# Hymba decoder block on one core: fewer places for TensorE's small products, states accumulated in PSUM, the diagonal blocks moved by nine transfers

## What is computed

```python
sa = -einsum('bhvk,bhk->bhv', S, kk_t)
S = S * w_t + sa[..., None] * b_t + v_t[..., None] * k_t
y = einsum('bhvk,bhk->bhv', S, r_t)
```

## Time and profile before

| | |
|---|---|
| median of three runs | 2065.28 us (2063.19 to 2066.71) |
| the profiled execution | 2057.9 us, its span 2056.1 us |
| TensorE | 1959.0 us busy, 15982 products |
| VectorE | 1251.0 us (61%) |
| ScalarE | 767.4 us (37%) |
| GpSimd | 369.9 us (18%) |
| DMA, hardware queue | 165456 packets, 32.5% of 16 engines |
| granted TensorE clock | 0.988 of full speed |

### The profile page before, as it was taken

How to read it: one execution, slowest core, us unless ns; L and a number is a source line. 1 busy time by engine, 2 the same in 40 slices (tenths; PEclk the granted TensorE clock), 3 DMA queues, 4 the chain that set the end, 5 groups by cost and what they waited for, 6 DMA issues and landing times.

```text
span 2056.1 us, 40076 instructions
## 1 busy us (share of the span) xinstructions
PE 1959.0 (95%) x15982; PEld 1549.3 (75%) x15982; DVE 1251.0 (61%) x2416; ACT 767.4 (37%) x1438; POOL 369.9 (18%) x672
## 2 busy tenths in 40 slices
PE   8999999999999998999999999999999899999995
PEld 5777777777777876777777777777777677887883
DVE  5657576675756676665757666675767655336434
ACT  6443334342424243434333424242424342334321
POOL 0001303021212121022131303121212122110112
PEclk9999999999999999999999999999999999999997
DMA  5532222222232224322222222222232433446443
GB/s 166 179 87 79 71 84 74 76 70 85 61 94 72 72 77 130 105 77 67 83 71 82 67 78 75 80 65 84 67 86 75 131 94 104 128 146 209 158 122 108
DMA packets 165643, 197.36 MB, mean 96 GB/s; under 512 B 70096, under 2 KB 73168, under 8 KB 165456
## 3 DMA queue, kind: packets, MB, share of 16 engines
q1 hardware_dynamic: 165456, 194.79, 32.5%
HBM read 174.79 MB, written 19.92 MB: 95 GB/s over the span
## 4 chain that ended last, share of the span: by engine, by line
PE 54%; DVE 11%; SPq 11%; POOL 10%; DMA 8%; issue 4%; ACT 2%; DVEq 0%; ACTq 0%; POOLq 0%
PE psum L1113 43%; SPq L358 6%; POOL xt L457 4%; POOL x L455 4%; SPq L353 3%; DMA x<-scratch_L 2%; SPq L337 2%; PE psum L1266 2%; DVE w_lo L695 2%; DMA w_raw<-in_w_in 2%; DMA scratch_X<-xt 2%; DMA scratch_L<-late 1%; ACT w_hi L513 1%; PE psum L1373 1%; DVE late L857 1%
## 5 line engine op out<-in xcount | busy, mean ns | idle before, releaser
L1113 PE MATMUL psum<-x_hi,w_hi 128*128 128x512 f32 x2144 | 895.1, 418 | 10.2 <-DVE x_lo L704 7.6
L1113 PE MATMUL psum<-x_hi,w_lo 128*128 128x512 f32 x2144 | 843.0, 393 | 0.0
L1113 PE MATMUL psum<-x_lo,w_hi 128*128 128x512 f32 x2144 | 840.3, 392 | 0.0
L513 ACT ACTIVATE w_hi<-w_raw 128x512 fp32r<-128x512 f32 x536 | 335.9, 630 | 1079.8 <-PE psum L1113 1003.9
L695 DVE TENSOR_TENSOR w_lo<-w_raw,w_hi 128x512 fp32r<-128x512 f32 x456 | 318.7, 700 | 504.1 <-ACT w_hi L513 488.6
L1113 PEld LDWEIGHTS psum<-x_hi,w_hi 128*128 128x128 f32 x2144 | 405.8, 189 | 129.2 <-issue 31.6
L1113 PEld LDWEIGHTS psum<-x_hi,w_lo 128*128 128x128 f32 x2144 | 404.9, 189 | 89.9
L1113 PEld LDWEIGHTS psum<-x_lo,w_hi 128*128 128x128 f32 x2144 | 406.3, 190 | 78.8 <-issue 7.7
L493 POOL TENSOR_TENSOR w_lo<-w_raw,w_hi 128x512 fp32r<-128x512 f32 x80 | 102.8, 1286 | 510.3 <-ACT w_hi L513 510.3
L953 DVE SCALAR_TENSOR_TENSOR states<-psum,pc,pt 128x64 f32<-128x64 f32 x112 | 31.7, 283 | 117.4 <-PE psum L1373 116.9
L449 POOL COPY xt<-sub_ident 64x256 f32<-64x256 f32 x16 | 6.3, 392 | 506.4 <-DMA x<-scratch_L 506.4
(11 more groups left out here) (240 smaller groups left out, 2035.7 us busy)
## 6 DMA issues: line engine op xcount, KB each, us to landing
w_raw<-in_w_in SPq DMA_DIRECT2D x408, 256.0 KB, 2.7
w_raw<-in_w_out SPq DMA_DIRECT2D x128, 256.0 KB, 2.6
stage<-in_x_t SPq DMA_DIRECT2D x20, 256.0 KB, 3.5
stage<-scratch_MIX SPq DMA_DIRECT2D x19, 256.0 KB, 4.0
x_t<-scratch_X SPq DMA_DIRECT2D x256, 4.0 KB, 1.6
scratch_MIX<-sa SPq DMA_DIRECT2D x16, 256.0 KB, 3.1
scratch_MIX<-ym SPq DMA_DIRECT2D x16, 256.0 KB, 3.4
lora<-in_x_t SPq DMA_DIRECT2D x16, 256.0 KB, 3.0
```

The lines of the kernel that those rows point to most:

```text
L513: return nc.scalar.activation(dst, src, ACT.Copy, scale=scale)
L1113: mm = nc.tensor.matmul(psum[:, s % 2], wt[gq % SPLIT][:, cols], xx[:, c], start=(c == 0 and wt is w_hi and xx is x_hi), stop=(c == KC - 1 ...
```

## The change

- `products` 0 moves from the middle of step 0 to step 1, in front of `products` 1, and the LoRA products of `channels` from step 2 to 1. `z` moves from step 6 to 5 behind the scores, level 0 from 12 to 11 behind the first values, `values` 1 from 15 to 14 in front of level 1, and level 2 from 15 to 14 behind it, into banks 2 and 3 (it waits for `kk_read`, their last reader, and no longer for level 1).
- VectorE masks both halves in step 1, ahead of the recurrence; its `level` 2 moves to step 14; the centring of y (`centre`) to the end of step 24.
- The fresh part stays in bank 6 unscaled. Each `chain` product adds to its columns there, and ScalarE (`chain`, an ACTIVATE with the scale `pc`) makes the next state: odd m ahead of `high`, even m behind it. `fresh`, `n_full`, `fresh_ready` and L939 go.
- Scratch `L`, `X` and a new `XT` hold whole 64x64 blocks with a gap of one row, so that `diagonal` addresses the 16x16 blocks as 64 rows of one stride. Transfers: 2 out, 1 in, 2 out, 4 back. Ahead of the loop four transfers write zeros to `X` and `XT`.
- All low parts are VectorE's.

```diff
@@ -265,13 +268,14 @@
-def pool_low(gq):
-    return any(j >= 1 and 19 <= at < 24 for j, at in current(gq - 4))
-def lows(gq, by_pool):
-    return sum(pool_low(x) == by_pool for x in range(gq + 1))
+def whole(name):
+    return scr[name].rearrange("(m r) -> m r", r=BLOCK_STEP)[:, 0:C * C].rearrange("m (s t) -> m s t", t=C)
+def diagonal(name):
+    places = scr[name].rearrange("(p r) -> p r", r=BLOCK_STEP * SUB // C)[:, 0:SUB * C]
+    return places.rearrange("p (s t) -> p s t", t=C)[:, :, 0:SUB]
@@ -290,8 +294,7 @@
             if gq >= RAW:
-                done = gq - RAW
-                sp.wait_ge(w_ready_pool if pool_low(done) else w_ready, lows(done, pool_low(done)))
+                sp.wait_ge(w_ready, gq - RAW + 1)
@@ -330,33 +333,28 @@
                 sp.wait_ge(a_read, 2 * i + 2)
-                for f in range(P // SUB):
-                    c = 1 if f < 4 else 0
-                    rows = slice(f * SUB, (f + 1) * SUB)
-                    cols = slice((f % 4) * SUB, (f % 4 + 1) * SUB)
-                    sp.dma_start(scr["L"][f].rearrange("m s t -> s m t"),
-                                 am[rows, :, :, c, 1 - c, cols].rearrange("s b h t -> s (b h) t")
+                for c in range(2):
+                    sp.dma_start(whole("L")[BH * c:BH * (c + 1)].rearrange("m s t -> s m t"),
+                                 am[us_rows(c), :, :, c, 1 - c].rearrange("s b h t -> s (b h) t")
...
-                sp.wait_ge(l_out, 8 * 16 * (i + 1))
+                sp.wait_ge(l_out, 2 * 16 * (i + 1))
...
-                sp.dma_start(sub_l, scr["L"].rearrange("f m s t -> (f m) s t")).then_inc(l_in, 16)
+                sp.dma_start(sub_l, diagonal("L")).then_inc(l_in, 16)
...
-                sp.dma_start(scr["X"].rearrange("f m x s t -> (f m) x s t"), sub_x).then_inc(x_out, 16)
+                if i == 0:
+                    sp.wait_ge(x_zero, 4 * 16)
+                sp.dma_start(diagonal("X"), sub_x[:, 0]).then_inc(x_out, 16)
+                sp.dma_start(diagonal("XT"), sub_x[:, 1]).then_inc(x_out, 16)
...
-                sp.wait_ge(x_out, 16 * (i + 1))
-                sp.wait_ge(pool_inited, 1)
-                for f in range(P // SUB):
-                    rows = slice(f * SUB, (f + 1) * SUB)
-                    cols = slice((f % 4) * SUB, (f % 4 + 1) * SUB)
-                    sp.dma_start(x16[rows, :, cols], scr["X"][f, :, 0].rearrange("m s t -> s m t")
+                sp.wait_ge(x_out, 2 * 16 * (i + 1))
+                for c in range(2):
+                    sp.dma_start(x16[us_rows(c)], whole("X")[BH * c:BH * (c + 1)].rearrange("m s t -> s m t")
...
-                    c = 1 if f < 4 else 0
-                    for hh in range(2):
-                        rows = slice(hh * HD + (f % 4) * SUB, hh * HD + (f % 4 + 1) * SUB)
-                        sp.dma_start(x16_t[rows, NB * c:NB * (c + 1), cols],
-                                     scr["X"][f, hh::2, 1].rearrange("b s t -> s b t")).then_inc(x_back, 16)
+                for hh in range(2):
+                    sp.dma_start(x16_t[head_rows(hh)], whole("XT")[hh::2].rearrange("m s t -> s m t")
+                                 ).then_inc(x_back, 16)
@@ -407,6 +405,11 @@
         load_up(1)
+        sp.wait_ge(pool_inited, 1)
+        for c in range(2):
+            for name in ("X", "XT"):
+                sp.dma_start(whole(name)[BH * c:BH * (c + 1)].rearrange("m s t -> s m t"), x16[us_rows(c)]
+                             ).then_inc(x_zero, 16)
@@ -640,6 +637,12 @@
+        def chain(i, m):
+            act.wait_ge(state_full, NCH * i + m + 1)
+            dst = states[:, m + 1] if m < NCH - 1 else state[:, i % PAIRS]
+            copy(dst, psum[:, 6, m * HD:(m + 1) * HD], pc[:, i % 2, m:m + 1]).then_inc(state_new, 1)
@@ -662,8 +665,14 @@
         for gq in range(QUARTERS):
+            for j, at in current(gq):
+                if j >= 1 and 21 <= at < 25:
+                    chain(j - 1, 2 * (at - 21) + 1)
...
+            for j, at in current(gq):
+                if j >= 1 and 20 <= at < 24:
+                    chain(j - 1, 2 * (at - 20))
@@ -907,7 +916,7 @@
             for x in range(2):
-                part_ = psum[:, (6, 6, 6, 4, 6)[lev] + x, 0:NB * C].rearrange("p (b t) -> p b t", b=NB)
+                part_ = psum[:, (6, 6, 2, 4, 6)[lev] + x, 0:NB * C].rearrange("p (b t) -> p b t", b=NB)
@@ -935,10 +943,6 @@
             dve.sem_inc(mt_ready, 1)
-            dve.wait_ge(n_full, i + 1)
-            then(nc.vector.tensor_tensor(fresh, psum[:, 6].rearrange("p (m d) -> p m d", d=HD),
-                                         pc[:, j].unsqueeze(2).broadcast_to([P, NCH, HD]), ALU.mult))
-            dve.sem_inc(fresh_ready, 1)
@@ -946,19 +950,15 @@
-        def chain(i, m):
-            n = i % PAIRS
-            dve.wait_ge(state_full, NCH * i + m + 1)
-            dst = states[:, m + 1] if m < NCH - 1 else state[:, n]
-            then(nc.vector.scalar_tensor_tensor(dst, psum[:, 7, 0:HD], pc[:, i % 2, m:m + 1], fresh[:, m],
-                                                ALU.mult, ALU.add))
-            dve.sem_inc(state_new, 1)
+        def centre(i):
+            spread = [P, BH, HD]
+            then(nc.vector.tensor_reduce(stat[:, 0], ym[:], AX, ALU.add))
+            then(nc.vector.tensor_scalar(stat[:, 0], stat[:, 0], -1.0 / HD, None, ALU.mult))
+            then(nc.vector.tensor_tensor(ym[:], ym[:], stat[:, 0].unsqueeze(2).broadcast_to(spread),
+                                         ALU.add))
+            dve.sem_inc(y_centred, 1)
...
-            if at == 0:
-                masked(i, 0)
-            if at == 1:
-                masked(i, 1)
@@ -976,8 +976,8 @@
                 level(i, 1)
+                level(i, 2)
...
-                level(i, 2)
@@ -993,10 +993,6 @@
                 transition(i)
-            if 21 <= at < 25:
-                chain(i, 2 * (at - 21) + 1)
-            if 20 <= at < 24:
-                chain(i, 2 * (at - 20))
@@ -1066,16 +1055,23 @@
         for gq in range(QUARTERS):
-            if gq + 4 < QUARTERS and not pool_low(gq + 4):
+            if gq + 4 < QUARTERS:
...
+                if j >= 1 and at == 1:
+                    masked(j - 1, 0)
+                    masked(j - 1, 1)
+            for j, at in current(gq):
...
+            for j, at in current(gq):
+                if j >= 1 and at == 24:
+                    centre(j - 1)
@@ -1101,7 +1097,7 @@
                 pe.wait_ge(tile_read, s - 1)
-            pe.wait_ge(w_ready_pool if pool_low(gq) else w_ready, lows(gq, pool_low(gq)))
+            pe.wait_ge(w_ready, gq + 1)
@@ -1123,7 +1119,7 @@
         def channels(j, at):
-            if at == 2:
+            if at == 1:
@@ -1272,12 +1268,12 @@
         def recurrence(i, at):
             if at == 1:
+                products(i, 0)
                 products(i, 1)
             if at == 3:
                 turns(i)
             if at == 5:
                 scores(i, 0)
-            if at == 6:
                 pe.wait_ge(t_read, 4 * i + 4)
                 mm = from_chunks(4, lambda b, c, hh: am[vs_rows(c), b, hh, c, 1 - c],
                                  lambda b, c, hh: uv[vs_rows(c), c, b, hh])
@@ -1287,19 +1283,18 @@
                 scores(i, 1)
             if at == 11:
                 values(i, 0)
-            if at == 12:
                 pe.wait_ge(s_read, 2 * i + 2)
-                pe.wait_ge(x_back, 24 * 16 * (i + 1))
+                pe.wait_ge(x_back, 4 * 16 * (i + 1))
                 from_chunks(6, masked_l, lambda b, c, hh: x16[us_rows(c), 2 * b + hh]).then_inc(lev_full, 1)
             if at == 13:
                 turn_p(i, 1)
             if at == 14:
+                values(i, 1)
                 pe.wait_ge(lev_read, 5 * i + 1)
                 from_heads(6, ym, x16_t).then_inc(lev_full, 1)
-            if at == 15:
-                values(i, 1)
-                pe.wait_ge(lev_read, 5 * i + 2)
-                from_heads(6, x16_t, ym).then_inc(lev_full, 1)
+                if i < INTERVALS - 1:
+                    pe.wait_ge(kk_read, i + 2)
+                from_heads(2, x16_t, ym).then_inc(lev_full, 1)
             if at == 16:
                 pe.wait_ge(lev_read, 5 * i + 3)
                 pe.wait_ge(mixa_ready, 2 * i + 2)
@@ -1332,8 +1327,8 @@
                                                   kbt[:, b, c, rows], uv[:, c, b, hh],
-                                                  start=True, stop=True, skip_group_check=True)
-                mm.then_inc(n_full, 1)
+                                                  start=(b == 0 and c == 0), stop=False,
+                                                  skip_group_check=True)
@@ -1366,12 +1361,10 @@
                 pe.wait_ge(mt_ready, i + 1)
-                pe.wait_ge(h_read, i + 1)
-                pe.wait_ge(fresh_ready, i + 1)
...
-            nc.tensor.matmul(psum[:, 7, 0:HD], mt[:, m], states[:, m], start=True, stop=True
-                             ).then_inc(state_full, 1)
```

(6 more changed lines are left out.)

24 lines of the change are left out of this document (5 added, 19 removed).

## The result

The median after is **1980.4 us** (1978.17 to 1982.50, 4 runs) against 2065.1 (2063.19 to 2066.71, 4 runs) before: ratio 0.959, 95% interval 0.9573 to 0.9607, so 84.7 us gained. Forecast were 2004.3 and the range 1990 to 2029; the kernel is faster, and faster than the range allowed. The profiled execution took 1980.56 us (span 1978.8, granted clock 0.991), 77.3 us less than that of before.

The account below looks back on a forecast made before the run. TensorE, busy 95% of the span, was taken as the bound. In us, joins 24.5, waits 22.9 + 3.6 + 2.4 and borders 8, less 0.4 at the start, made 61 off 2065.3: 2004.3, range 1990 to 2029.

Parts of the forecast that it names:

- joins: TensorE's small groups moved beside neighbours: 0.37 us saved in one tile shape, 0.21 across shapes, 24.5 us in all.
- borders: At the two changes to a new half of x, fewer TensorE waits for VectorE's states: 8 us, bounds 0 and 18.
- rival 1: Waits come back elsewhere, VectorE nearly full in steps 12 to 14, inverse norm tight before step 12's transposes: 2026, chance 0.12.
- 22.9 + 3.6 + 2.4: TensorE's waits that go, in us: level 0 for its transfer, turn of step 13, level 2 for level 1's reader.
- taking off the same 61 from 2065.3: Last step: the gain worked out on the profiled run (2057.9 us) applied to the median, giving 2004.3.
- 11 x 0.33 = 3.6: Turn of step 13: eleven waits for `softmax_norm` go, as the weight load no longer stands behind 24 issues: 3.6 us.
- Step 9, put at nothing: The other 16 `softmax_norm` waits, at step 9, hang on ScalarE's exponentials and stay.
- Level 2: At step 14, no longer waits for level 1's reader but for `kk_read`: 2.4 us gained, 5 us cost at worst.
- The landing: Returned blocks: 11.5 us earlier by fewer issues, less 3 for larger transfers; 3 us of cover before level 0.
- it fits: ScalarE's queue takes the chain's states, perhaps 0.3 us each, around the high part: nothing on TensorE.
- The low parts: nothing: Steps 19 to 23: VectorE takes over 80 low parts, 0.70 us each, without its state steps: no effect.
- The interval: Each of the 16 intervals expected 3 to 4 us shorter.

Follow-up runs that it names:

- experiment 1: The kernel before with only the nine new transfers (scratch layout, issues and waits of the change): 2015.8 us, ratio 0.9759.
- 2: The changed kernel with all joins undone, the six groups at their old steps, transfers and states as changed: 2000.9 us, ratio 0.9691.
- the first lot: The timing lot in which runs of the kernel before stood beside four of the follow-up kernels; before's median there was 2065.4 us.
- experiment 8: The changed kernel with step 9 reordered, scores of the second half ahead of the turned probabilities of the first: 1972.2 us, ratio 0.9568.
- experiment 5: The changed kernel with the chain's states back on VectorE, the low parts staying there too: 2010.4 us, ratio 0.9745.
- experiment 4: The changed kernel with the old 34 transfers instead of the nine: 2059.3 us, ratio 0.9962.
- 6: The changed kernel with the five low parts of steps 19 to 23 back on GpSimd: 1980.9 us, ratio 0.9608.
- experiment 7: The changed kernel with the states back on VectorE and the five low parts back on GpSimd: 1989.0 us, ratio 0.9654.

## Why the prediction missed

| term | forecast | distances | medians |
|---|---|---|---|
| transfers: level 0, turn 13, level 2 | 28.9 | 38.1 (before, 1) | 49.6 |
| joins | 24.5 | 22.3 (2, after) | 20.5 |
| borders, start, all else | 7.6 | 11.6 (1, 2) | 14.9 |
| outside the groups: the clock | 0 | 5.3 | |
| before's median above its profiled run | 0 | 7.4 | |
| sum | 61 | 84.7 | 85.0 |

(In brackets the two kernels compared. The medians' column goes from 2065.4, before in the first lot, over 2015.8 and 2000.9 to 1980.4.)

Nearly every mechanism of the forecast was there, and no rival came (the tight fit that rival 1 named shows only in the kernel of experiment 8). The time missed the forecast by 23.9 us, and 20.7 of them are in one row, the transfers.

- **The step that failed is the price of the waits for the transfers, "22.9 + 3.6 + 2.4".** It takes a us of waiting in the table for a us of time. Experiment 1 took these waits away alone: 38.1 us by the distances and 49.6 by the medians, for 28.9. Of the 38.1, level 0 is 24.7 for 22.9, turn 13 is 6.8 for 3.6, level 2 is 3.0 for 2.4, and step 9, which was said to stay, is 2.8. A wait costs more than its length even at the full clock: 0.2 us more at step 13 (experiment 1), less than 0.1 at level 2 (0.30 us for 0.23 to 0.24), 0.26 in the chain of experiment 5 (0.48 us for 0.22). And behind some of the long ones TensorE runs at the lower clock.
- **The clock.** Before, some of TensorE's waits for level 0 were followed by stretches at 1.2 GHz; its timeline:

```profile
664.01 0.69 PE L1257 MATMUL psum<-x,late 64*64 64x64 f32 x32 [2.03 <-DMA x_t<-scratch_X]
...
666.12 0.63 PE L1113 MATMUL psum<-x_hi,w_hi 128*128 128x512 f32 x1
666.55 0.63 PE L1113 MATMUL psum<-x_lo,w_hi 128*128 128x512 f32 x1
```

  The large products are 0.43 us apart instead of 0.23, after four of the sixteen waits (2.0 to 2.4 us long), and after none of the twelve others (0.35 to 1.76). That waits bring such stretches is shown by experiments 1 and 4: outside the groups there are 39 spacings at half the clock before, 15 with the waits gone (experiment 1, none of them at a level 0) and 84 with longer waits (experiment 4, clock 0.979). How often it happens differs from run to run: the 13 runs of before in the first lot spread from 2059.3 us (granted clock 0.990) to 2073.3 (0.984), and the slower ones have the lower clock. With the wait gone the four runs lie within 4.3 us at 0.990 to 0.991, and the profiled one is at the median. The prediction's last step, "taking off the same 61 from 2065.3", took the 7.4 us between the profiled run (2057.9, 0.988) and the median for something that both kernels have. They are gone after the change. About 4 us of them are the clock by an estimate (the median clock of the 13 runs is 0.986: 0.002 x 2057); the rest is open, and medians of the same kernel differed by up to 5 us between the lots. So 5 us are the clock in the profiles, and perhaps 4 more in the medians.
- **"11 x 0.33 = 3.6".** The eleven waits make 4.1 us, so the reading was near. What it left out is the 0.2 us on top of each; the groups of step 13 fell by 6.8.
- **Step 9, put at nothing.** The prediction said that its sixteen waits hang on ScalarE's exponentials and stay. They made 12.0 us before (one of them below), 9.1 with the nine transfers, 7.8 after the whole change and 9.4 when the old transfers came back (experiment 4), so they hung on the transfers in part. By what way is open.

```profile
987.39 1.09 PE L1098 MATMUL psum<-cst,score 128*128 128x128 f32 x8 [0.82 <-DVEq L897]
```

- **Level 2, the right size for the wrong reason.** Its wait of 2.4 us went with the transfers alone (experiment 1), with the old banks and the old reader. That it waits for `kk_read` now gained nothing that a run shows, and cost nothing: at most 0.3 us an interval was feared, and its group costs 2.32 to 2.34 us in nearly every interval.
- **The joins**: 0.37 for one shape against 0.40 (12.7 / 32) and 0.33 (5.2 / 16); 0.21 across shapes against 0.20 for `z`. Level 0 behind the values gave 0.12: it had stood beside the transposes of step 12, and the four interruptions fewer were counted, the old neighbour was not. The extrapolation from 64x64 to 64x128 tiles, which no row showed, held.
- **The landing**: 11.5 us saved less 3 for the larger transfers, and 3 us of cover, were forecast. The cover was 3.6 us, but two misses cancel in it. In the interval of the rows, the time from the first issue of the blocks to the last landing fell from 1001.75 - 963.09 = 38.7 us to 953.9 - 922.45 = 31.5, so 7.2 earlier: the larger transfers took 4.3 of the 11.5, not 3. In return the blocks leave 1.1 us earlier before level 0 is asked for (957.51 - 922.45 = 35.1 us, against 997.1 - 963.09 = 34.0), for which the sum had nothing.
- **The states**: "it fits", at 0.3 us each. 313 ns, no wait of a chain product, spacing 1.60. "The low parts: nothing" is right as well (6), and for the reason given, that VectorE has no state steps there any more: with them it costs 15 to 21 us (experiment 5 against 7).
- **The borders**: 8 forecast. No chain product waits for ScalarE's states there; the chain's 12.1 us of waits went whole, its distances (lone products) by 14.4; the bonus product took back 8.5 by its distances (7.6 by the table), at the two borders as foreseen. Together with the smaller groups there 10 to 11.6.
- **The interval**: 3 to 4 us shorter was expected. Inside a half of the tokens level 0 stood 96.0 to 98.9 us apart before; now the next one behind that of 957.51 is

```profile
1050.37 0.69 PE L1253 MATMUL psum<-x,late 64*64 64x64 f32 x32
```

  92.86 apart, so 3.1 to 6.0 shorter.

Of the 14.9 us in the row "all else", 8.3 to 8.6 are the states at the borders (experiment 7); about 6 are not assigned: the masks ahead of the recurrence, the centring and the scaling that went had no runs of their own.

The range was too narrow on the fast side: its near bounds were worked out from costs that might be nothing, and none of them stood for a wait that costs more than its length.

## What to carry to other kernels

Where TensorE is busy 95% of the time, a wait is worth more than its length (up to 0.3 us more here, at the full clock), and a wait of 2 us or more for a transfer can bring half-speed products behind it: look at the spacing of the products behind it, and at the granted clock of several runs, before taking the table's sum for the price. Price a moved product by its shape and its old neighbours as well as its new ones, in distances between the starts of the large products around it; that held to 10% here, over all joins, for shapes that had not been seen together. And look at what stands ahead of a serial chain's reader in its queue: 0.69 us of somebody else's work there cost 15 to 21 us, on an engine at 64%, and an order of two products that no engine's load would suggest gave 8.
